# Forming the first adaLN modulation on TensorE, tile by tile, with two projection blocks accumulating along

## What is computed

```
mod  = silu(c) @ w_ada[l] + b_ada[l]        # 6 x 1024 columns, also for c_ctx
h    = x * (1 + scale1) + shift1            # modulated input of the mixer
p    = h @ w_in[l]                          # q, k, v of two attentions, z, xbc, dt
a, b = window attention, global attention;  c = bidirectional SSD
y    = concat(a, b, c) @ w_out[l]
x    = layer_norm(alpha * x + gate1 * y)
x    = layer_norm(alpha * x + gate2 * swiglu(x * (1 + scale2) + shift2))
```

## Time and profile before

| | |
|---|---|
| median of 3 runs | 3884.65 us (3880.82 to 3886.8) |
| span of the profiled execution | 3878.7 us, 6 us below the median; its own time is not recorded apart from the span |
| busy: PE, PEld, DVE, ACT, POOL | 3426.3 (88%), 2858.7 (74%), 1871.5 (48%), 853.1 (22%), 1411.6 (36%) us |
| TensorE clock granted, mean | 0.945 of full speed |
| layer 0 "ab" stage | about 53 to 207 us |
| layer 1 "ab" stage | up to 2265 us |

### The profile page before, as it was taken

How to read it: one execution, slowest core, us unless ns; L and a number is a source line. 1 busy time by engine, 2 the same in 40 slices (tenths; PEclk the granted TensorE clock), 3 DMA queues, 4 the chain that set the end, 5 groups by cost and what they waited for, 6 DMA issues and landing times. The chain is left out here.

```text
span 3878.7 us, 48787 instructions
## 1 busy us (share of the span) xinstructions
PE 3426.3 (88%) x17688; PEld 2858.7 (74%) x17688; DVE 1871.5 (48%) x2851; ACT 853.1 (22%) x1566; POOL 1411.6 (36%) x1019
## 2 busy tenths in 40 slices
PE   0969989877959999999996779999888789999997
PEld 0849988755838888888884549988656578888884
DVE  8977533687682222222228887534675522222125
ACT  1135432213050001000004126432211211010102
POOL 1343112243353333343334342103253444444443
PEclk9989999988979999999997879989978899999998
DMA  7500001002301111111102410001002011111111
GB/s 275 172 12 1 1 29 59 11 17 97 109 27 38 38 38 38 32 43 38 38 27 88 157 49 1 0 27 60 6 19 84 28 44 46 51 43 50 47 49 49
DMA packets 63853, 197.67 MB, mean 51 GB/s; under 512 B 6160, under 2 KB 16656, under 8 KB 62736
## 3 DMA queue, kind: packets, MB, share of 16 engines
q1 hardware_dynamic: 54736, 172.32, 13.5%
q10 hardware_dynamic: 9024, 24.14, 1.7%
HBM read 177.05 MB, written 19.40 MB: 51 GB/s over the span
## 5 line engine op out<-in xcount | busy, mean ns | idle before, releaser
L188 PE MATMUL ps<-h_hi,f_whi 128*128 128x512 f32 (+1 forms) x1760 | 652.0, 370 | 50.7 <-POOL h_lo L1911 25.2
L189 PE MATMUL ps<-h_lo,f_whi 128*128 128x512 f32 (+1 forms) x1760 | 651.1, 370 | 0.0
L190 PE MATMUL ps<-h_hi,f_wlo 128*128 128x512 f32 (+1 forms) x1760 | 650.3, 369 | 0.0
L2096 DVE TENSOR_TENSOR f_gated<-f_gated,ps 128x512 f32<-128x512 f32 (+1 forms) x110 | 69.8, 634 | 1006.9 <-PE ps L190 1006.9
L1993 POOL TENSOR_TENSOR f_whi<-f_wraw,small 128x1024 fp32r<-128x1024 f32 x128 | 242.7, 1896 | 569.4 <-PE ps L190 569.4
L2104 DVE SCALAR_TENSOR_TENSOR x_res<-ps,mod,x_res 128x512 f32<-128x512 f32 (+1 forms) x440 | 306.9, 698 | 242.1 <-PE ps L190 241.8
L188 PEld LDWEIGHTS ps<-h_hi,f_whi 128*128 128x128 f32 x1760 | 334.1, 190 | 109.5 <-issue 42.7
L190 PEld LDWEIGHTS ps<-h_hi,f_wlo 128*128 128x128 f32 x1760 | 333.6, 190 | 56.1
L189 PEld LDWEIGHTS ps<-h_lo,f_whi 128*128 128x128 f32 x1760 | 334.0, 190 | 55.5
L188 PE MATMUL ps<-f_ahi,f_whi 128*128 128x512 f32 (+1 forms) x880 | 328.3, 373 | 0.0
L189 PE MATMUL ps<-f_alo,f_whi 128*128 128x512 f32 (+1 forms) x880 | 323.5, 368 | 0.0
(11 more groups left out here) (218 smaller groups left out, 6484.3 us busy)
## 6 DMA issues: line engine op xcount, KB each, us to landing
f_wraw<-in_w_ffn SPq DMA_DIRECT2D x132, 512.0 KB, 3.6
ada_w<-in_w_ada SPq DMA_DIRECT2D x80, 512.0 KB, 4.0
wrawc<-in_w_in SPq DMA_DIRECT2D x26, 512.0 KB, 4.1
wrawab<-in_w_in SPq DMA_DIRECT2D x16, 512.0 KB, 4.5
wrawo<-in_w_out SPq DMA_DIRECT2D x16, 512.0 KB, 3.9
ada_w<-in_w_ada ACTq DMA_DIRECT2D x16, 512.0 KB, 4.3
x_res<-in_xT SPq DMA_DIRECT2D x8, 640.0 KB, 6.6
x_spill<-x_res ACTq DMA_DIRECT2D x8, 640.0 KB, 5.1
```

Source lines behind the costliest of these rows:

```text
L188: pe.matmul(out, w_hi, h_hi, start=first, stop=False)
L189: pe.matmul(out, w_hi, h_lo, start=False, stop=False)
L190: return pe.matmul(out, w_lo, h_hi, start=False, stop=last)
L2096: dve.tensor_tensor(g, g, pl.bank(3 + c, tn), ALU.mult).then_inc(u_taken[c], 1)
```

## The change

In layer 0 the stage `load_inputs` and the lead `modulate_inputs` are gone; a class `FirstInputs` takes their place inside `project_attention`. w_ada for shift1 and scale1 comes in another layout (`w_first`), contraction on the partitions, so that TensorE forms the modulation: for each tile k of h 2 x 8 matmuls of a 128x128 weight tile with the two conditioning columns, in full float32 (new L352). VectorE adds the bias, ScalarE and VectorE both form h from x (ScalarE rounds while it does), VectorE takes the rest. Blocks 0 and 1 of w_in are multiplied tile by tile behind each k (`multiply_two`), in all six banks at once; the other two banks take the modulation's columns in turn. GpSimd has no part in it, and blocks 2 to 7 go as before. Both modulated copies leave x as it is: alpha is applied later, in the output projection of layer 0, by ScalarE to x as it is loaded from the input a second time; nothing is spilled.

In both layers the hardware loops of `project_attention` are written out, ScalarE copies the turned v instead of VectorE, and VectorE's 64 dot products are one loop.

```diff
+class FirstInputs:
+    SLOTS = 6
+    def sync(self, sp, load_block):
+        sp.dma_start(self.cond[:, :, :], a["cond_cols"]).then_inc(self.cond_in, 16)
+        sp.dma_start(pl.bada[:, :], a["b_ada"][0]).then_inc(self.bias_in, 16)
+        for k in range(KT):
+            for j in range(2):
+                n = 2 * k + j
+                if n >= self.SLOTS:
+                    sp.wait_ge(self.formed, n - self.SLOTS + 1)
+                sp.dma_start(self.w[n % self.SLOTS][:, :, :], a["w_first"][k, j]) \
+                    .then_inc(self.w_in[n % self.SLOTS], 16)
+            sp.dma_start(pl.x[:, k, :], a["xT"][:, k, :]).then_inc(self.x_in[k], 16)
+            if k < 2:
+                load_block(k)
+        sp.wait_ge(self.biased, 2 * KT)
+    def tensor(self, pe, multiply):
+        def form(k):
+            for j in range(2):
+                n = 2 * k + j
+                pe.wait_ge(self.w_in[n % self.SLOTS], 16 * (n // self.SLOTS + 1))
+                for i in range(KT):
+                    mm = pe.matmul(self.columns(k)[:, 2 * j:2 * j + 2], self.w[n % self.SLOTS][:, i, :],
+                                   self.cond[:, i, :], start=(i == 0), stop=(i == KT - 1))
+                mm.then_inc(self.formed, 1)
+        pe.wait_ge(self.cond_ready, 1)
+        form(0)
+        form(1)
+        for k in range(KT):
+            pe.wait_ge(self.rest, k + 1)
+            multiply(k)
+            if k + 2 < KT:
+                form(k + 2)
+    def scalar(self, act, round_block):
...
+        for k in range(KT):
+            act.wait_ge(self.biased, 2 * k + 2)
+            act.wait_ge(self.x_in[k], 16)
+            for (t0, t1), who in (((0, SEQ), 0), ((SEQ, TOK), 1)):
+                act.activation(pl.hi[:, k, t0:t1], pl.x[:, k, t0:t1], ACT.Identity,
+                               scale=pl.mod[:, SC1 + k, who:who + 1],
+                               bias=pl.mod[:, SH1 + k, who:who + 1]).then_inc(self.rounded, 1)
+            if k < 2:
+                round_block(k)
+    def vector(self, dve, split_block):
...
+        for k in range(KT):
+            dve.wait_ge(self.formed, 2 * k + 2)
+            for j, t in ((0, SC1 + k), (1, SH1 + k)):
+                dve.tensor_scalar(pl.mod[:, t, :], self.columns(k)[:, 2 * j:2 * j + 2], pl.bada[:, t:t + 1],
+                                  1.0 - j, ALU.add, ALU.add).then_inc(self.biased, 1)
...
+            for (t0, t1), who in (((0, SEQ), 0), ((SEQ, TOK), 1)):
+                dve.tensor_scalar(self.tmp[k % 3][:, t0:t1], pl.x[:, k, t0:t1],
                                   pl.mod[:, SC1 + k, who:who + 1], pl.mod[:, SH1 + k, who:who + 1],
+                                  ALU.mult, ALU.add).then_inc(self.scaled, 1)
+            rest_of(k)
+            if k < 2:
+                split_block(k)
...
 def project_attention(pl, l, last, lead):
         @block.sync
+            if by_tile:
+                lead.sync(sp, load)
+                sp.dma_start(pl.const[:, :], a["consts"]).then_inc(consts_in, 16)
...
         @block.tensor
+            def multiply_two(k):
+                if k == 0:
+                    pe.wait_ge(ring.ready, 4)
+                for n in range(2):
+                    for c in ORDER:
+                        t0, tn = CHUNKS[c]
+                        mm = three_pass(pe, pl.bank(3 * n + c, tn), ring.hi[n][:, k, :], ring.lo[n][:, k, :],
+                                        pl.hi[:, k, t0:t0 + tn], pl.lo[:, k, t0:t0 + tn],
+                                        k == 0, k == KT - 1)
+                        if k == KT - 1:
+                            mm.then_inc(full[c], 1)
...
         @block.scalar
+                if at.kind == "v":
+                    for g, c in enumerate(ORDER):
+                        t0, tn = CHUNKS[c]
+                        act.wait_ge(turned, at.i * 3 + (g + 1))
+                        tt = slice(t0 // P, (t0 + tn) // P)
+                        act.activation(pl.v[:, tt, :].rearrange("p t (g d) -> p t g d", g=2)[:, :, at.i, :],
+                                       pl.bank(6 + (at.i * 3 + g) % 2, tn).rearrange("p (t d) -> p t d", d=P),
+                                       ACT.Copy).then_inc(stored, 1)
...
         @block.vector
-            with dve.Fori(0, 2) as i:
-                with dve.Fori(0, 4) as j:
-                    ada.sums(dve, i * 4 + j)
...
-                    dve.tensor_copy(pl.v[:, tt, :].rearrange("p t (g d) -> p t g d", g=2)[:, :, i, :],
+            with dve.Fori(0, 8) as r:
+                ada.sums(dve, r)
             ada.finish(dve)
...
 def gather_mix(pl, l, last):
-        sp.dma_start(pl.x[:, :, 0:width], pl.x_dram[:, :, 0:width]).then_inc(x_in, 16)
+        src = pl.a["xT"] if l == 0 else pl.x_dram
+        sp.dma_start(pl.x[:, :, 0:width], src[:, :, 0:width]).then_inc(x_in, 16)
...
+        if l == 0:
+            act.wait_ge(x_in, 16)
+            for k in range(KT):
+                act.activation(pl.x[:, k, :], pl.x[:, k, :], ACT.Copy, scale=ALPHA).then_inc(kept, 1)
```

More of the change, by code:

```diff
@@ L302, in other_modulation @@
     return Modulation(pl, l, G1, 6 * KT, SC2)
[L307 to L335, removed]
@@ L359, in vector @@
                                   pl.mod[:, SC1 + k, who:who + 1], pl.mod[:, SH1 + k, who:who + 1],
-                                  ALU.mult, ALU.add).then_inc(scaled, 1)
-            dve.wait_ge(scaled, 2 * k + 2)
-            dve.tensor_scalar(pl.x[:, k, :], pl.x[:, k, :], ALPHA, None, ALU.mult).then_inc(kept, 1)
[L363 to L369, removed]
-            act.activation(pl.hi[:, k, :], tmp[k % 3][:, :], ACT.Copy).then_inc(rounded, 1)
-            act.wait_ge(kept, k + 1)
-            act.dma_start(pl.x_dram[:, k, :], pl.x[:, k, :]).then_inc(spilled, 16)
-        act.wait_ge(spilled, KT * 16)
@@ L467, in project_attention @@
     tag = f"ab{l}"
+    kinds = ["q0", "q1", "k", "v"] * 2
+    by_tile = isinstance(lead, FirstInputs)
     chunks_of = lambda kind: (0, 1) if last and kind in ("q0", "q1") else ORDER
-    segments = [(2, ["q0", "q1", "k", "v"])]
+    blocks = [At(n, n % 2, kinds[n], n // 4, n % 4, n // 2,
+                 sum(2 in chunks_of(k) for k in kinds[:n])) for n in range(8)]
     ring = Ring(pl, tag)
@@ L480, in _ @@
         def _(sp):
-            load = lambda at: ring.load(sp, at, a["w_in"][l, at.n])
-            over(sp, [(1, ["w", "w"])], lambda kind: (), load)
+            load = lambda n: ring.load(sp, blocks[n], a["w_in"][l, n])
+            if by_tile:
+                lead.sync(sp, load)
+                sp.dma_start(pl.const[:, :], a["consts"]).then_inc(consts_in, 16)
+            else:
+                load(0)
+                load(1)
             ada.start(sp)
@@ L486, in _ @@
             sp.dma_start(pl.prm[:, :], a["prm"][l]).then_inc(prm_in, 16)
-            def body(at):
-                load(at)
-                ada.load(sp, at.n - 2)
-            over(sp, [(3, ["w", "w"])], lambda kind: (), body, start=2)
+            for n in range(2, 8):
+                load(n)
+                ada.load(sp, n - 2)
             for r in (6, 7):
@@ L498, in _ @@
             pool.sem_inc(ring.ready, 2)
-            lead.gpsimd(pool)
-            over(pool, [(3, ["w", "w"])], lambda kind: (), lambda at: ring.split(pool, at, full[1]), start=2)
+            if not by_tile:
+                lead.gpsimd(pool)
+            for n in range(2, 8):
+                ring.split(pool, blocks[n], full[1])
         @block.tensor
@@ L523, in _ @@
                 act.sem_inc(taken[c], 2)
-            ring.round_first(act)
-            lead.scalar(act)
+            if by_tile:
+                lead.scalar(act, lambda n: ring.round_block(act, n))
+            else:
+                ring.round_first(act)
+                lead.scalar(act)
             ada.silu(act)
-            def body(at):
+            for at in blocks:
                 for c in ORDER:
@@ L1663, in vector @@
         dve.wait_ge(x_in, 16)
+        if l == 0:
+            dve.wait_ge(kept, KT)
     return Lead({c: [(rest, len(items))] for c in range(3)}, tensor, scalar, vector, sync=sync)
```

108 lines of the change are left out of this document (63 added, 45 removed).

## The result

The changed kernel takes 3895.07 us, the median of 18 runs (3882.41 to 3909.52); before takes 3884.77 us in the same measurement (18 runs, 3880.09 to 3892.16). The ratio of the two is 1.0024, 95% interval [1.0015, 1.0033]: slower by a quarter of a per cent, where 1% faster was predicted. The profiled execution took 3894.88 us.

What follows compares the result with a forecast made beforehand. VectorE's modulation sums, not TensorE, were taken to end both attention projections. Gains of 36.1 (layer 0) and 5.9 (layer 1), less 1.2 (output projection) and 1.0 (norm stage), make 39.8 us: median 3844.9, range 3832 to 3864.

Steps and rivals of the forecast that it cites:

- Forming: Layer 0's start: 16 small fp32 matmuls a tile at 0.12 us each, 1.9 us a tile, double at the low clock.
- rival B: Layer 0's tile-by-tile phase: clock stays low, last form ends at 82.8, gain only 10 us, time 3875; 12%.
- The sum for layer 0: First stage: second modulation's sums start at 64.1 and end at 170.5, next stage at 171.8 instead of 207.86; gain 36.1 us.
- Layer 1: Attention projection: VectorE loses two groups of v copies, its sums still set the end; gain 5.9 us, bounds 3 and 8.
- Output projections: Layer 0's output projection: scaling x on ScalarE delays later loads and first sums; cost 1.2 us, bounds 0 and 6.5.
- the second step that failed: Output projections: VectorE meeting GpSimd's split got no cost; only less meeting, a little more than 2 us, counted in layer 0.
- The norm stage behind the projection: Behind layer 0's projection: it meets TensorE at its low clock; cost 1 us, bounds 0 and 3.
- the spill: Spill of x, behind VectorE's work in a stretch that is gone: costed at nothing.
- the written-out loops: Unrolled loops: costed at nothing, as no row shows a wait at a loop's end.

Runs made afterwards that it cites:

- e8: Changed kernel with GpSimd's split held until VectorE's scalings end, and only four of eight contraction steps in each form: 3862.3 us, one run.
- e3: Changed kernel with TensorE forming all eight tiles of the modulation first and multiplying all eight afterwards: 3874.1 us, ratio 0.9962.
- e2: Changed kernel with one wait: in both output projections GpSimd splits only after VectorE has scaled all of mix_c: 3877.1 us, ratio 0.9973.
- e5: Kernel before with GpSimd's split held, ScalarE's v copies, alternating banks and written-out block loop, without the new start: 3879.0 us, ratio 0.9982.
- e10: Changed kernel unedited, run again for a second trace: 3899.9 us, one run.
- e1: Kernel before with one wait: in both output projections GpSimd splits only after VectorE has scaled all of mix_c: 3884.5 us, ratio 0.9992.
- e9: Changed kernel, split held, forms first, constants early, VectorE forming the scale half, conditioning loaded once: 3851.7 us, ratio 0.9907.
- e12: e9 with TensorE forming one tile further ahead, before the first product: 3842.6 us, ratio 0.9896.
- e6: Changed kernel, split held, each tile's small matmuls cut in two halves, one after each block's product: 3874.0 us, ratio 0.9986.
- e11: e6 unedited, run again for a second trace: 3887.8 us, one run.

## Why the prediction was wrong

**Forming (the step that failed).** I took 0.12 us for a small matmul, from the earlier trace rows, reading "x10 in 1.23 us" as ten calls. They were five: a plain fp32 call leaves two records, as the 256 records of the changed kernel's 128 small calls show. A call costs two times 0.112 us at the high clock (e8: 16 records in 1.84) and two times 0.214 at the low one (e3). That puts a tile's form at 3.6 us at best instead of 1.9. The range counted with 0.06 to 0.12 a call and so left out the true 0.22 and 0.43. e8, in which the forms cost what I had taken for them, starts its next stage 3.6 us behind my forecast.

**The clock.** I gave 12% to rival B, the clock low tile by tile, with 10.7 us a tile and the last form at 82.8; they were 10.2 us and 85.7. In part that is luck: B took 3.8 us for the forms, twice the mis-read price, where they took 4.4, mostly at the high clock, and 6.9 for the products, which took 5.8. Against B stood "while a tile takes double, TensorE has no pause". It has none now either (70.7 of 73.1 us busy), and yet the clock falls. The rule of the Trainium skill that I cited (TensorE: Matmul & The Clock Gate, "Why this matters for your kernels") has the clock swing at each contraction tile of a thin product that waits for its transfers. The swing at each tile is what this trace shows, every 10.2 us, but without such a wait, and e2's first tiles do without the swing; 12% was too little. My premise for it, a third of a tile's time in thin matmuls, was itself too low by the mis-read price: it is half (3.6 of 7.07 us at the high clock).

**The sum for layer 0**, 36.1 predicted and 0.8 measured (207.86 - 207.04). The first product came at 24.5 instead of 18.6: +5.9, mostly since at the low clock the first two forms took 13.8 us. The six tiles behind it took 61.2 us (24.5 to 85.7) instead of 34.4: +26.8, of which 6 x 1.7 = 10 is the second record of each call (7.07 us a tile for my 5.4) and the rest the clock. From the last form to the first sum it was 11.9 instead of 11.1, the sums took 107.9 instead of 106.4, and from their end to the next stage 1.5 instead of 1.3: +2.5. Together 35.2.

**Layer 1.** 5.9 predicted, 5.2 measured; e5, which has the projection's edits without the new start, has 5.5. That the sums set the end of both projections, and TensorE's 21.6 us wait would only move to the end of the stage, was right.

**Output projections.** Predicted a cost of 1.2 from the scaling of x; e2 shows none. (My own terms, 6 less 3.4 of slack less a little more than 2, leave at most 0.6 and not 1.2.) What cost 16 us here I hadn't seen, though I had read that VectorE's scaling takes 1.14 us alone and 3.8 beside GpSimd. The same pair meets in two further stages, and there I never asked which engine gives way. It is the second step that failed, a term that I put at nothing without a reason. Without it the change is 0.3% faster than before (e2), so the sign of my forecast turned on it; its size turned on the forms.

**The other terms.** The norm stage behind the projection cost 0.5 in the traced run and 1.9 in e10 and e2 (1.0 predicted). No run varied the spill or the written-out loops by themselves; e5 keeps the spill and has the loops written out, and neither projection of it is longer than e1's. The attention stage's 5.1 us of the changed trace are chance, as e1 shows.

## To carry to other kernels

Count an operation's records against the program's calls before taking a price from "x10": a plain fp32 matmul here is two, each with its own weight load. Thin matmuls put between products aren't always paid in their own time alone: in the traces of the changed kernel they took the clock from the products beside them, and with half as many (one trace each of e8, e9 and e12) the tiles ran at the high clock almost throughout, once it had risen at 24 to 32 us. So make few of them, and give the rest to an engine that waits. Where a scaling on VectorE meets a split on GpSimd, fix the order with a wait: it was free in the kernel before and worth 16 us in the changed one.

## What was not expected of the hardware

- Which engine gives way when VectorE and GpSimd meet was in these traces one way or the other for a whole stretch, not in between: VectorE's 20 scalings took 5.3 or 12.9 us. GpSimd started 1.8 us behind VectorE before (950.88 - 949.05) and 1.4 behind it in the changed kernel (954.14 - 952.77), in layer 1 likewise 1.9 (2950.68 - 2948.82) and 1.5 (2957.84 - 2956.37), and every trace of the changed start without the held split (four) had the dear outcome in both layers. That the 0.4 us decide is only argued; no run varied it alone, and why the start moved in layer 1, whose stage the change doesn't touch, is open.
- TensorE stayed at the low clock through 54.7 us of back-to-back small matmuls (e3), and one program had its clock high from 27.8 us on in one trace and from 59.8 in the other (e6, e11). What decides it stays open, as does how often; the spread of the e6 runs, 3859 to 3892, goes with it but also with the attention stage.
- The column of the granted clock reads 1.00 up to the first change of the clock in each trace (93.9 us before, 29.4 in the changed kernel, 65.9 in e3), while the matmuls there are spaced as at the low clock (0.43 us for 512 columns). At the start of a program the spacing has to be read, not the column.
